# Mixture-of-experts tail of a two-block model: expert units skewed by one more step, more down projections in plain f32, the first tile's tokens by a one-hot matmul

## The reference

```
def hierarchical_moe(x, w_rg, b_rg, w_re, b_re, w_up, w_down):   # x: 512 x 1024
    group_p = softmax(x @ w_rg + b_rg)                 # 4 groups, the best one is taken
    in_group = (x @ w_re + b_re) of the chosen group   # 4 experts, the best two are taken
    gate = weights of the two experts, zeros elsewhere # 16 experts
    h = einsum('nd,edf->nef', x, w_up)                 # per expert 1024 -> 2 x 256
    h_g, h_u = split(h, 2, axis=-1)
    h = silu(h_g) * h_u * gate[:, :, None]
    return einsum('nef,efd->nd', h, w_down)            # per expert 256 -> 1024
...
f = hierarchical_moe(x, ...)
x = layer_norm_2(ALPHA * x + f, ln2_g, ln2_b)
```

## Time and profile before

| | us |
|---|---|
| median of 3 runs | 2854.38 (2852.93 to 2854.75) |
| profiled execution, its own time | 2851.48 |
| its span, first to last instruction | 2849.7 |
| first expert matmul begins | 2536.25 |
| last down projection ends | 2837.92 |
| PE busy over the span | 2504.5 (88%) |
| ACT, DVE busy | 947.0, 1158.4 |
| mean granted TensorE clock | 0.937 |

### The profile page before, as it was taken

One profiled execution on the slowest core, in us unless ns is written; L12 is line 12 of the kernel. 1 busy time (PEld: TensorE's weight loads), 2 busy tenths in 40 slices (PEclk: granted clock), 3 DMA queues, 4 the chain that ended last, 5 costly groups with the idle time before them and its releaser, 6 DMA issues. The chain is left out here.

```text
span 2849.7 us, 31839 instructions
## 1 busy us (share of the span) xinstructions
PE 2504.5 (88%) x12838; PEld 1504.4 (53%) x12838; DVE 1158.4 (41%) x1626; ACT 947.0 (33%) x1280; POOL 486.6 (17%) x208
## 2 busy tenths in 40 slices
PE   4869979999996779799999987879999989968887
PEld 3733623333335544533333335658777878646665
DVE  3876221212114966311121226664222031457766
ACT  3345311111113436211111116663332352255554
POOL 0422000000000612000000003224333534100000
PEclk7989989999997889899999998989999999979999
DMA  9510569999998400569999975212233312168885
GB/s 310 200 61 1 200 255 382 410 410 410 410 406 300 176 0 32 234 248 409 410 410 409 409 283 146 69 49 89 74 96 111 116 62 89 41 251 321 294 298 191
DMA packets 276227, 646.26 MB, mean 227 GB/s; under 512 B 12048, under 2 KB 110606, under 8 KB 276110
## 3 DMA queue, kind: packets, MB, share of 16 engines
q1 hardware_dynamic: 269614, 633.88, 59.5%
q0 software_dynamic: 2592, 7.87, 0.8%
q10 hardware_dynamic: 3904, 2.88, 0.3%
HBM read 639.88 MB, written 6.29 MB: 227 GB/s over the span
## 5 line engine op out<-in xcount | busy, mean ns | idle before, releaser
L701 PE MATMUL ps<-ring,scr 128*64 128x512 f32 x1952 | 426.4, 593 | 5.4 <-DMA ring<-in_w_up 3.8
L1366 POOL TENSOR_TENSOR raw_r<-raw,w_high 128x2048 fp32r<-128x2048 f32 (+1 forms) x62 | 276.4, 4463 | 464.1 <-ACT w_high L1580 464.1
L701 PEld LDWEIGHTS ps<-ring,scr 128*64 128x64 f32 x1952 | 138.2, 137 | 282.3 <-issue 271.2
L422 POOL TENSOR_TENSOR one_hot_T_r<-hy,one_hot_T_r 128x1024 fp32r<-128x1024 f32 x16 | 38.6, 2409 | 1133.0 <-ACT one_hot_T_r L926 1133.0
L723 PE MATMUL ps<-ring,scr 128*64 128x512 f32 x1024 | 226.8, 595 | 1.4 <-ACT scr L912 1.4
L1381 PE MATMUL ps<-x_high,w_high 128*128 128x512 f32 x480 | 198.3, 413 | 6.2 <-DVE xT_r L1760 5.4
L1382 PE MATMUL ps<-xT_r,w_high 128*128 128x512 f32 x480 | 190.9, 398 | 0.0
L2362 DVE TENSOR_TENSOR ring_r<-ring,ring_high 128x2048 fp32r<-128x2048 f32 x70 | 159.5, 2288 | 72.8 <-ACT ring_high L2234 72.2
L1383 PE MATMUL ps<-x_high,raw_r 128*128 128x512 f32 x480 | 188.8, 393 | 0.0
L976 DVE SCALAR_TENSOR_TENSOR one_hot_T<-h_tok,convw,one_hot_T 128x512 f32<-128x512 f32 x170 | 183.0, 1076 | 9.0
L1143 DVE SCALAR_TENSOR_TENSOR xT<-ps,mod,xT 128x512 f32<-128x512 f32 x128 | 86.8, 744 | 217.7 <-PE ps L689 216.7
(11 more groups left out here) (512 smaller groups left out, 4734.2 us busy)
## 6 DMA issues: line engine op xcount, KB each, us to landing
ring<-in_w_down SPq DMA_DIRECT2D x64, 2048.0 KB, 17.0
ring<-in_w_up SPq DMA_DIRECT2D x62, 2048.0 KB, 20.1
ring<-in_w_gate SPq DMA_DIRECT2D x60, 2048.0 KB, 16.7
ring<-in_w_up SPq DMA_DIRECT2D x56, 1024.0 KB, 5.6
ring<-in_w_ada SPq DMA_DIRECT2D x22, 2048.0 KB, 10.5
ring<-in_w_down SPq DMA_DIRECT2D x28, 1024.0 KB, 5.2
raw<-in_w_in SPq DMA_DIRECT2D x24, 1024.0 KB, 5.1
raw<-in_w_in SPq DMA_DIRECT2D x20, 512.0 KB, 5.4
```

The source lines that it names most:

```text
L701: mm = pe.matmul(ps[CAP * half:CAP * (half + 1), 1 + j // 2, :], x_e[:, at_x:at_x + CAP], weights[:, k, half * HALF:(half + 1) * HALF], st ...
L1366: pool.tensor_tensor(dst, src, high.bitcast(F32), ALU.subtract).then_inc(w_ready, 1)
```

## The change

Five edits, all in `sparse`:
1. `PLAIN` is (0, 1, 2) rather than (1, 3): 21 of the 28 down projections take plain f32 operands, and expert 3 is the split one.
2. PE runs `down(n - 2)` between the halves of `up(n)`, and `turn_hid(n - 1)` behind them; before, `turn_hid(n - 1)` stood between the halves and `down(n - 1)` behind them. The chunks' order, and the order of the splits on ACT and DVE, are rewritten to go with it. The transposes of the next tile's tokens stand in the loop at n % 4 = 1, before at n % 4 = 2. A split down chunk is split one step later, behind `keep_hidden`.
3. `finish_y` takes two passes over the 1024 columns rather than three.
4. The first tile's tokens are no longer taken from the gather: 32 f32 matmuls of `xtok` with a one-hot matrix `hot0` (one new DVE product) put them transposed into PSUM. They stand ahead of the small matmul that yields `idx_i`. The gather of tile 0 stays, for the residual.
5. SP loads a tile's group into a register just before the tile's first chunk, before all 7 ahead of the first chunk.

```
-PLAIN = (1, 3)
+PLAIN = (0, 1, 2)
...
-    for n in range(UNITS + 1):
-        out += [("up0", n), ("up1", n)] if n < UNITS else []
-        out += [("down", n - 1)] if n >= 1 else []
+    for n in range(UNITS + 2):
+        out += [("up0", n)] if n < UNITS else []
+        out += [("down", n - 2)] if n >= 2 else []
+        out += [("up1", n)] if n < UNITS else []
...
@@ SP
-            which = [sp.value_load(...) for i in range(TILES)]
+            which = []
             for q, (kind, n) in enumerate(order):
                 i, e = group_tile(n)
+                if i == len(which):
+                    which.append(sp.value_load(...))
...
@@ PE
+            pe.wait_ge(row_kept, 2 * TT)
+            pe.wait_ge(hot0_ready, 1)
+            for half in range(2):
+                for b in range(4):
+                    kt = 4 * half + b
+                    for t in range(TT):
+                        mm = pe.matmul(ps[:, 6 + half, b * P:(b + 1) * P], xtok[:, t, kt * P:(kt + 1) * P], hot0[:, t, :], start=(t == 0), stop=(t == TT - 1))
+                mm.then_inc(xt_mm, 1)
             pe.wait_ge(disp_ready, 1)
...
-            turn_tokens(0)
-            for n in range(UNITS + 1):
+            for n in range(UNITS + 2):
                 if n < UNITS:
                     up(n, 0)
-                if n >= 1:
-                    turn_hid(n - 1)
-                if n % PER_GROUP == 2 and n // PER_GROUP + 1 < TILES:
-                    turn_tokens(n // PER_GROUP + 1)
+                if n >= 2:
+                    down(n - 2)
                 if n < UNITS:
                     up(n, 1)
-                if n >= 1:
-                    down(n - 1)
+                if 1 <= n <= UNITS:
+                    turn_hid(n - 1)
+                if n < UNITS and n % PER_GROUP == 1 and n // PER_GROUP + 1 < TILES:
+                    turn_tokens(n // PER_GROUP + 1)
...
@@ ACT, the new loop
+            for n in range(UNITS + 2):
+                for half in range(2):
+                    if n + 1 < UNITS:
+                        split(f"up{half}", n + 1)
+                if n >= 6 and n % PER_GROUP == 2:
+                    y_deviation(n // PER_GROUP - 1)
+                if n < UNITS:
+                    act.wait_ge(chunk_used, place["up1", n] + 1)
+                    act.activation(sg[n % 2], ps[:, n % 2, 0:FF2], ACT.Silu).then_inc(sg_ready, 1)
+                if 1 <= n <= UNITS:
+                    keep_hidden(n - 1)
+                    if is_split("down", n - 1):
+                        split("down", n - 1)
+                if n < UNITS and n % PER_GROUP == 1 and n // PER_GROUP + 1 < TILES:
+                    keep_tokens(n // PER_GROUP + 1)
...
@@ DVE
+            dve.tensor_tensor(hot0, hot, oht[:, :, 0:1].to_broadcast([P, TT, P]), ALU.mult).then_inc(hot0_ready, 1)
...
-                op(dve.tensor_scalar(yt[i % 2], yt[i % 2], V["mv"][:, 0:1], V["rstd"], ALU.subtract, ALU.mult))
-                op(dve.tensor_tensor(yt[i % 2], yt[i % 2], gain_row, ALU.mult))
-                dve.tensor_tensor(yt[i % 2], yt[i % 2], bias_row, ALU.add).then_inc(y_ready, 1)
+                op(dve.scalar_tensor_tensor(yt[i % 2], yt[i % 2], V["mv"][:, 0:1], gain_row, ALU.subtract, ALU.mult))
+                dve.scalar_tensor_tensor(yt[i % 2], yt[i % 2], V["rstd"], bias_row, ALU.mult, ALU.add).then_inc(y_ready, 1)
```

More of the change, by code:

```diff
@@ L1935 @@
 RING = 7
-PLAIN = (1, 3)
+PLAIN = (0, 1, 2)
 ROUTE = dict(bg=20, lgT=P, gl=TT * 20, ex=16, gpad=28, a=64, b=16, c=16, d=16, top=4, rest=4, ptop=4, prio=4, thr=4, i128=6, irow=7,
              ng=4, cmp=16, tiles=4, tend=4, cmp7=21, tgf=7, toff=4, sl=16, slot=4, ge=24, tidx=4, pos=4, oht=28, vals=24, mov=168,
-             dsp=42, df=7, row=P, upper=P, hot=TT * P, stats=12, mv=2, rstd=1)
+             dsp=42, df=7, row=P, upper=P, hot=TT * P, hot0=TT * P, stats=12, mv=2, rstd=1)
 def group_tile(n):
@@ L1978, in sparse @@
     mov = V["mov"].rearrange("p (t i c) -> p t i c", t=TT, i=TILES)
-    hot = V["hot"].rearrange("p (t n) -> p t n", t=TT)
+    hot, hot0 = (V[n].rearrange("p (t n) -> p t n", t=TT) for n in ("hot", "hot0"))
     dsp = V["dsp"].rearrange("p (i c) -> p i c", i=TILES)
@@ L1982, in sparse @@
     place = {c: q for q, c in enumerate(order)}
[L1983 to L1987, removed]
+    split_order = [("up0", 0), ("up1", 0)]
+    for n in range(UNITS + 1):
+        split_order += [("up0", n + 1), ("up1", n + 1)] if n + 1 < UNITS else []
+        split_order += [("down", n - 1)] if n >= 1 and is_split("down", n - 1) else []
+    split_no = {c: q + 1 for q, c in enumerate(split_order)}
     g_small, g_rows = sem("g_small"), sem("g_rows")
@@ L1994, in sparse @@
         sem(n) for n in ("group_ready", "count_mm", "tg_ready", "disp_ready", "disp_mm", "idx_ready", "dest_ready"))
-    row_mm, row_kept, rows_out = sem("row_mm"), sem("row_kept"), sem("rows_out")
+    row_mm, row_kept, rows_out, hot0_ready = sem("row_mm"), sem("row_kept"), sem("rows_out"), sem("hot0_ready")
     slot_in = [sem(f"ring3_in{i}") for i in range(RING)]
@@ L2030, in _ @@
             sp.wait_ge(tg_ready, 1)
-            which = [sp.value_load(tg_i[0:1, i:i + 1], min_val=0, max_val=EXP_GROUPS - 1) for i in range(TILES)]
+            which = []
             for q, (kind, n) in enumerate(order):
                 i, e = group_tile(n)
+                if i == len(which):
+                    which.append(sp.value_load(tg_i[0:1, i:i + 1], min_val=0, max_val=EXP_GROUPS - 1))
                 if q >= RING:
@@ L2129, in turn_tokens @@
                 pe.wait_ge(xg_in[i % 2], 16 * (i // 2 + 1))
[L2130 to L2133, removed]
+                pe.wait_ge(xl_ready, 2 * i)
                 for half in range(2):
@@ L2248, in y_deviation @@
                 act.activation(V["rstd"], V["mv"][:, 1:2], ACT.Sqrt, bias=eps).then_inc(y_root, 1)
-            for half in range(2):
-                split(f"up{half}", 0)
+            split("up0", 0)
             keep_tokens(0)
-            for n in range(UNITS + 1):
-                if n >= 5 and n % PER_GROUP == 2:
-                    y_deviation(n // PER_GROUP - 1)
[L2256 to L2263, removed]
+            split("up1", 0)
+            for n in range(UNITS + 2):
[3 more added lines that the diff above has]
+                if n >= 6 and n % PER_GROUP == 2:
+                    y_deviation(n // PER_GROUP - 1)
                 if n < UNITS:
@@ L2266, in _ @@
                     act.activation(sg[n % 2], ps[:, n % 2, 0:FF2], ACT.Silu).then_inc(sg_ready, 1)
-                    if is_split("down", n):
-                        split("down", n)
+                if 1 <= n <= UNITS:
[4 more added lines that the diff above has]
+                    keep_tokens(n // PER_GROUP + 1)
             y_deviation(TILES - 1)
@@ L2332, in _ @@
             oht = V["oht"].rearrange("p (t i) -> p t i", t=TT)
-            step(dve.tensor_tensor(oht, wide(tidx, TILES), V["irow"].unsqueeze(1).to_broadcast([P, TT, TILES]), ALU.is_equal))
+            op(dve.tensor_tensor(oht, wide(tidx, TILES), V["irow"].unsqueeze(1).to_broadcast([P, TT, TILES]), ALU.is_equal))
+            dve.tensor_tensor(hot0, hot, oht[:, :, 0:1].to_broadcast([P, TT, P]), ALU.mult).then_inc(hot0_ready, 1)
             dve.wait_ge(g_exp, 1)
@@ L2350, in _ @@
             dve.tensor_tensor(mov, oht.unsqueeze(3).to_broadcast([P, TT, TILES, 6]), vals.unsqueeze(2).to_broadcast([P, TT, TILES, 6]), ALU.mult).then_inc(disp_ready, 1)
[L2351 to L2356, removed]
             def split_rest(kind, n):
@@ L2373, in keep_y @@
                     dve.wait_ge(stored[i % 2], 16 * (i // 2))
+                dve.wait_ge(xg_in[i % 2], 16 * (i // 2 + 1))
                 for half in range(2):
@@ L2387, in finish_y @@
                 dve.wait_ge(y_root, i + 1)
-                op(dve.reciprocal(V["rstd"], V["rstd"]))
-                op(dve.tensor_scalar(yt[i % 2], yt[i % 2], V["mv"][:, 0:1], V["rstd"], ALU.subtract, ALU.mult))
-                op(dve.tensor_tensor(yt[i % 2], yt[i % 2], gain_row, ALU.mult))
-                dve.tensor_tensor(yt[i % 2], yt[i % 2], bias_row, ALU.add).then_inc(y_ready, 1)
-            for half in range(2):
-                split_rest(f"up{half}", 0)
-            tokens_rest(0)
[L2396 to L2405, removed]
+                step(dve.reciprocal(V["rstd"], V["rstd"]))
+                op(dve.scalar_tensor_tensor(yt[i % 2], yt[i % 2], V["mv"][:, 0:1], gain_row, ALU.subtract, ALU.mult))
+                dve.scalar_tensor_tensor(yt[i % 2], yt[i % 2], V["rstd"], bias_row, ALU.mult, ALU.add).then_inc(y_ready, 1)
+            split_rest("up0", 0)
+            tokens_rest(0)
+            split_rest("up1", 0)
+            dve.wait_ge(disp_mm, 1)
+            op(dve.tensor_copy(V["dsp"], ps[:, 2, 0:6 * TILES]))
+            dve.tensor_copy(idx_i, dsp[:, :, 0]).then_inc(idx_ready, 1)
+            op(dve.tensor_scalar(V["df"], dsp[:, :, 1], -4096.0, 4096.0, ALU.mult, ALU.add))
```

(18 more changed lines are left out.)

## The result

The changed kernel takes 2869.03 us (median of 4 runs, 2866.99 to 2872.55) against 2853.65 for the kernel before: a ratio of 1.0056, 95% interval 1.0038 to 1.0073. It is slower by 15.4 us. The forecast was 2857.9, 3.5 more than before; the time is inside its range of 2843 to 2874, and nearer to rival C (2877) than to the forecast.

What follows compares the result with a forecast made beforehand. PE's stretch of expert matmuls in the last stage, 301.7 us with its waits and low clock, was taken as the bound; -9.6 + 5.2 - 32.9 + 12.6 + 4.9 + 22.0 + 3.3 - 1.2 - 0.8 = +3.5 gave 2857.9, range 2843 to 2874.

Steps and rivals of the forecast that it cites:

- rival C: Gathers meet weight traffic and land after 8 us rather than 4.2: +19, 2877; decides from about 5 us; chance 0.18.
- Start: First expert matmul at 2526.7 rather than 2536.25, by one-hot matmuls and earlier first weight chunk: -9.6 us.
- Plain for split: Seven more down projections plain instead of split, 0.74 us each on PE: +5.2 us.
- Waits that go: PE's waits ahead of split down projections, for `keep_y` and `hidT_low`, end: -32.4 us, and 0.5 for the last.
- Wait (a) and (b): PE waits for the tile's split down chunk: 2.1 us in six tiles, +12.6, and +4.9 in the last.
- Wait (c): PE's token transposes wait for the gather, landing after 4.2 us: 4.4 us in five tiles, +22.0.
- Clock: Stretches at the lower clock level behind PE's waits cost 16 us, before 17.2: -1.2 us.
- End: Final norm behind the last tile takes two passes rather than three: -0.8 us.
- A tile's period: Time per tile in the expert loop: 36.9 us of work, 43.4 with the waits, before 43.1.
- B: Rival, faster: waits as worked out, but low clock behind them shrinks from 16 us to 4: 2846; chance 0.22.
- E: Rival: the start gives less, one-hot passes taking 0.225 us each: +4.7, 2863; chance 0.11.
- D: Rival: no wait for split down chunks or gathered tokens, -12.6 - 22.0 and some 10 of clock: 2813; chance 0.04.

Runs made afterwards that it cites:

- the run with the start alone: Kernel before with only the one-hot matmul for the first tile's tokens and the late register loads: 2844.17 us, ratio 0.9969.
- all plain: Changed kernel with both repairs and every down projection plain, PLAIN = (0, 1, 2, 3): 2811.23 us, ratio 0.9848 to the kernel before.
- both repairs: Changed kernel with next tile's tokens transposed one unit later and the split down chunk made a step earlier: 2802.1 us, ratio 0.9830 to the kernel before.

## Why the prediction was right or wrong

**Right in the waits, too small in one term.** Three waits were forecast to take the place of those removed, and all three are there. The change came out at +15.4 rather than +3.5; that the time is inside the range is due to the range having been drawn wide enough for rival C.
- Start: -9.6 forecast, -9.1 in the trace, -9.3 by the run with the start alone.
- Plain for split: +5.2 of work forecast. At a granted clock of 1.00 throughout, PE's busy time was 264.4 with all plain and 259.4 with three of four: +5.0 for seven more. That the edit pays by the `hidT_low` waits alone was not said: it gives -9.6 without a skew.
- Waits that go: both kinds are gone, -32.4.
- Wait (a) and (b): +17.5 forecast, 16.3 listed.
- Wait (c), the tokens: this is the mis-sized term. The prediction took the median landing of before, 4.2, and so "4.4 us, in five tiles". Its other links hold: the gather starts 5.8 us behind the split down projection (2721.11 to 2726.88), where 5.9 was worked out, and 0.3 behind `keep_y`. But rival C had itself counted the slots that PE frees just ahead and SP's chunks for them. The landing was 7.1. The listed waits are 37.7, forecast 22.0 in five tiles and 2.5 at the start; the start's was 2.6, so the five are 7.0 each rather than 4.4. That is 13.2 too little, more than the whole 15.4 - 3.5 = 11.9 by which the forecast was short; the other terms together were slightly too high. Holding the two chunks back brought 4.2 and 2856.45.
- Clock: 16 forecast. By subtraction in the trace, 326.0 - 257.3 (work of 21 plain and 7 split units with six sets of tokens) - 54.5 (waits listed: 37.7, 16.3, 0.5) = 14.2. Each token wait was followed by a stretch at the lower level, as the prediction had it for long waits; the 14.2 is what is left over, and not a count of these stretches.
- End: -0.8 forecast, -0.9.
- A tile's period was to be 43.4; it is 326.0 / 7 = 46.6, which is again the token wait.

**The rivals.** C, given 0.18, is what happened, at 7.1 rather than 8: its condition, landing above 5 us, holds. The Trainium skill's rule (DMA: Bandwidth & Descriptors, section on SWDGE, HWDGE and iDMA: the two kinds of queue are separate inside a DMA engine, which serves them in turn) pointed to a later landing, and the landing was later, but the trace does not agree with the way in which the estimate used it. By the estimate the gather's data would have taken twice as long beside a chunk, 1.4 us more. In the trace they took no longer, and the 2.9 more stand ahead of the gather's first packet, while the weights' packets pass. Why they pass first is open. The chances leaned to slower, 0.39, but the single time took in neither the rule nor C. The row chosen for the landing was the wrong neighbour: of the seven gathers of before, five had their packets almost to themselves, with no chunk issued nearer than 2.5 us, and gave the median; the two at the start, issued among the first chunks, had the largest, 8.9. B and E did not happen, and D only with both repairs.

## What to carry to other kernels

When a step is moved closer to the transfer that feeds it, price the transfer with what will be on the DMA engines at its new moment, not with the median of the old one: what PE frees just ahead of it is what the queue will send beside it. A skew that gives one wait more room takes room from another, so list for each instruction it moves what must be ready and when, transfers and buffer releases included. Edits made together can hide each other: four of these were worth 21 us and the fifth lost 36, and two steps moved turned the whole into a gain of 51. A skew is not good or bad as such: this one cost 36 us in one place and was worth 31 in another.

## What the runs showed of the hardware

A gather of 0.5 MB landed after a median of 4.2 us when no weight chunk was issued nearer to it than 2.5 us, and after 7.1 us with one chunk of 1 MB issued some 3 us ahead and one at the same moment; holding these two back restored 4.2. The delay stood ahead of the gather's first packet, which came 4.1 to 4.4 us after the issue rather than 1.6 to 1.7, while its packets took some 2.2 us in either case. A wait of PE of some 7 us was each time followed by 3 to 4 us of work at the 1.2 GHz level; in the kernel with both repairs, where no wait in the stretch is over 2 us, the granted clock was 1.00 throughout. And 32 f32 matmuls of 128 columns ran as 64 passes in 7.38 us, 0.115 us each.
